# A wider slot block for the second expert of a pair in a mixture-of-experts layer

## The reference

```
logits = x @ router_w + router_b
top_val, top_idx = lax.top_k(logits, 2)
top_w = softmax(top_val)
for e in range(8):
    y = y + combine[..., e:e+1] * ((silu(x @ w_gate[e]) * (x @ w_up[e])) @ w_down[e])
```

## Time and profile before

| | before |
|---|---|
| median of 3 runs | 1698.21 us (1696.55 to 1700.08) |
| profiled execution, its own time | 1697.78 us |
| its span, first to last instruction | 1696.0 us |
| mean granted TensorE clock | 0.965 |
| PE busy | 1553.1 us (92%) |
| DVE busy / ACT busy | 398.8 us / 317.5 us |
| moved by DMA | 518.13 MB, 305 GB/s over the span |
| chain that ended last: PE / DMA / SP's queue | 46% / 18% / 4% |

### The profile page before, as it was taken

One profiled execution on the slowest core, in us unless ns is written; L12 is line 12 of the kernel. 1 busy time (PEld: TensorE's weight loads), 2 busy tenths in 40 slices (PEclk: granted clock), 3 DMA queues, 4 the chain that ended last, 5 costly groups with the idle time before them and its releaser, 6 DMA issues.

```text
span 1696.0 us, 33539 instructions
## 1 busy us (share of the span) xinstructions
PE 1553.1 (92%) x15321; PEld 1035.7 (61%) x15323; DVE 398.8 (24%) x781; ACT 317.5 (19%) x618; POOL 44.1 (3%) x83
## 2 busy tenths in 40 slices
PE   5996999979977999999999999988999899899986
PEld 4775788868765665766665656544565554565552
DVE  4666545465664300000000001000010000100002
ACT  3553444334541000100000001000010000000001
POOL 2010000010110000000000000000000000000000
PEclk8997899989987999999999999999999999999999
DMA  8523355356217898999999999999999999999994
GB/s 269 193 89 110 129 193 198 124 174 212 100 59 264 311 372 316 333 366 394 394 394 394 394 395 391 384 397 392 397 387 391 392 387 397 384 395 390 392 388 177
DMA packets 219575, 518.13 MB, mean 305 GB/s; under 512 B 6944, under 2 KB 8992, under 8 KB 219440
## 3 DMA queue, kind: packets, MB, share of 16 engines
q1 hardware_dynamic: 217248, 510.74, 81.0%
q0 software_dynamic: 1920, 5.31, 1.0%
q10 hardware_dynamic: 272, 0.00, 0.0%
HBM read 514.98 MB, written 1.05 MB: 304 GB/s over the span
## 4 chain that ended last, share of the span: by engine, by line
PE 46%; DMA 18%; SPq 4%; DVE 2%; issue 1%; ACT 0%; DVEq 0%; ACTq 0%
PE B L1844 23%; PE B L1859 16%; DMA ring<-in_moe_w_down_dram 16%; SPq L417 4%; PE B L1829 2%; PE B L1898 2%; DMA ring<-in_moe_w_up_dram 1%; PE B L1869 1%; DMA raw<-in_moe_w_down_dram 1%; PE B L1882 1%; PE B L1522 0%; PE B L1523 0%; PE B L1524 0%; DVE stats L891 0%; DVE acc L1455 0%
## 5 line engine op out<-in xcount | busy, mean ns | idle before, releaser
L1844 PE MATMUL B<-ring,xt 128*32 128x128 f32 (+1 forms) x5248 | 358.4, 325 | 15.4 <-DMA ring<-in_moe_w_up_dram 13.9
L1844 PE MATMUL B<-raw,xt 128*32 128x128 f32 (+1 forms) x4608 | 307.9, 322 | 19.7 <-DMA raw<-in_moe_w_up_dram 8.8
L1844 PEld LDWEIGHTS B<-ring,xt 128*32 128x32 f32 (+1 forms) x5248 | 247.0, 123 | 122.4 <-issue 24.0
L1844 PEld LDWEIGHTS B<-raw,xt 128*32 128x32 f32 (+1 forms) x4608 | 217.0, 122 | 109.4 <-issue 29.3
L1438 DVE TENSOR_TENSOR hact<-hact,B 128x256 f32<-128x256 f32 (+1 forms) x105 | 36.7, 383 | 884.1 <-ACT hact L799 884.1
L1859 PE MATMUL B<-ring,hidt 128*32 128x256 f32 (+1 forms) x1600 | 212.7, 479 | 17.9 <-DMA ring<-in_moe_w_down_dram 17.6
L870 DVE TENSOR_TENSOR wl<-raw,wh 128x1024 fp32r<-128x1024 f32 (+2 forms) x144 | 157.6, 1118 | 109.9 <-ACT wh L567 109.6
L1522 PE MATMUL B<-wh,xth 128*128 128x512 f32 (+1 forms) x416 | 168.6, 405 | 15.6 <-DVE wl L870 12.5
L1523 PE MATMUL B<-wl,xth 128*128 128x512 f32 (+1 forms) x416 | 163.9, 394 | 0.0
L1524 PE MATMUL B<-wh,xtl 128*128 128x512 f32 (+1 forms) x416 | 163.2, 392 | 0.0
L1859 PEld LDWEIGHTS B<-ring,hidt 128*32 128x32 f32 (+1 forms) x1600 | 75.7, 122 | 139.9 <-issue 104.0
(11 more groups left out here) (312 smaller groups left out, 947.2 us busy)
## 6 DMA issues: line engine op xcount, KB each, us to landing
ring<-in_moe_w_up_dram SPq DMA_DIRECT2D x46, 2048.0 KB, 19.7
ring<-in_moe_w_down_dram SPq DMA_DIRECT2D x44, 2048.0 KB, 19.5
raw<-in_moe_w_gate_dram SPq DMA_DIRECT2D x40, 2048.0 KB, 22.1
ring<-in_moe_w_gate_dram SPq DMA_DIRECT2D x30, 2048.0 KB, 20.7
raw<-in_moe_w_down_dram SPq DMA_DIRECT2D x26, 2048.0 KB, 19.1
raw<-in_moe_w_up_dram SPq DMA_DIRECT2D x24, 2048.0 KB, 19.8
raw<-in_w_in_dram SPq DMA_DIRECT2D x12, 2048.0 KB, 8.0
raw<-in_dense_w_gate_dram SPq DMA_DIRECT2D x5, 2048.0 KB, 7.7
```

What stands on the lines that cost most here:

```text
L1844: last = pe.matmul(bank[g * b.w:(g + 1) * b.w, o:o + b.cols], xt[:, k, b.c0:b.c0 + b.w], w[:, k, g * b.cols:(g + 1) * b.cols], start=k == ...
```

## The change

The second stream of PAIR gets a second block, of 32 slots, so that both streams have 96 slots in the same two blocks. The gather for a PAIR takes 192 columns in four banks, where it took 160 in three. The result takes bank 7 too, and the caps of streams 5 and 7 are 96 where they were 64.

```diff
-    CAPS = (96, 192, 32, 32, 96, 64, 96, 64)
+    CAPS = (96, 192, 32, 32, 96, 96, 96, 96)
...
         PAIR = Kind([[Block_(64, 0, 0, 0, 256, 0, 0, 4, 0), Block_(32, 64, 1, 0, 128, 1, 0, 5, 0, 64, 32)],
-                     [Block_(64, 96, 2, 0, 256, 2, 0, 6, 0, 0, 224)]],
-                    [[(0, 256, 0), (1, 128, 1)], [(2, 256, 2)]], (0, 1, 2), 3)
+                     [Block_(64, 96, 2, 0, 256, 2, 0, 6, 0, 0, 224), Block_(32, 160, 3, 0, 128, 3, 0, 7, 0, 64, 96)]],
+                    [[(0, 256, 0), (1, 128, 1)], [(2, 256, 2), (3, 128, 3)]], (0, 1, 2, 3), 2)
...
                 pick_stream(0, 96, first)
-                pick_stream(96, 64, second).then_inc(pick_done, 1)
+                pick_stream(96, 96, second).then_inc(pick_done, 1)
```

## The result

| | before | after |
|---|---|---|
| median | 1697.87 us (4 runs, 1696.55 to 1700.08) | 1526.4 us (4 runs, 1526.32 to 1529.08) |
| ratio | | 0.8993, 95% interval 0.8977 to 0.9008 |
| profiled execution / its span | 1697.78 / 1696.0 us | 1526.32 / 1524.2 us |

The kernel is 10.1% faster, 171.5 us by the medians. The forecast was 1527 us.

What follows compares the result with a forecast made beforehand. The prediction took transfers to bound the PAIR passes before and PE after. Start 1005.27, PAIR 253.52, one turn 246.49, tail 19.42 and 1.78 outside gave 1526.5, forecast as 1527 us, range 1514 to 1546.

Steps and rivals of the forecast that it cites:

- What bounds the kernel before: PAIR pass and both turns: transfers set the pace, 31.84 us a chunk against 27.76 us of PE work.
- The number of passes: Loop: 65 tokens over 64 slots cause the second turn; with 96 slots it goes, 225.20 us less.
- The wide chunk: Chunks of the two remaining PAIR passes: PE work rises 6.04 us to 33.80 us, and PE becomes the bound.
- SOLO's price: Added block of 32 behind a block of 64 in one unit: 1.96 us, the price the forecast took.
- The two prices: A block of 32 costs 1.96 us in SOLO or 1.77 us in a stream by itself; the cheaper makes chunks 33.23 us.
- What the waits absorb: PAIR chunks: 4.1 of the 6.0 us of added work fill waits, and 2.0 us a chunk lengthen the pass.
- Once a pass: Work once per PAIR pass after the change: gather 5.33 us, turned weights 2.77 us, scatter 7.1 us.
- The sum: Whole kernel: PAIR starts at 1005.27, then PAIR 253.52, one turn 246.49, tail 19.42, outside 1.78: 1526.5, so 1527 us.
- The first rival: PAIR passes: added blocks disappear in the waits and passes stay at the transfers' pace, 1474 us; chance 0.04.
- The second: PAIR passes: PE is the bound but waits for landings stay on top, 1556 us; chance 0.08.
- The third: Loop still turns twice and wide blocks are paid in three passes, 1778 us, 80 us slower; chance 0.02.
- The rate: Transfers in the two remaining PAIR stretches: down to some 350 to 370 GB/s.

Runs made afterwards that it cites:

- the cut in bytes: Down units of the PAIR passes load three of their four slices, PE work unchanged: 1654.19 us on the kernel before, 1527.91 us on the kernel after.
- the caps alone: Kernel before with only the caps changed and no added blocks, so expert 4's 65th token is left out: 1471.99 us, ratio 0.8664.
- the turned order: Kernel after with stream 1's blocks reversed (32 ahead of 64) on gate and up units: 1521.84 us, against 1527.08 us for the kernel after beside it.
- the turn put back: Kernel after with one more loop turn, empty of tokens: 1786.37 us, ratio 1.053.
- the kernel with the narrow PAIR: Kernel after with 64 slots again in the second stream of the PAIR pass ahead of the loop, the loop staying wide: 1500.03 us, ratio 0.8838.

## Why the prediction was right

- **What bounds the kernel before**: the transfers, shown by the cut in bytes, which moved the kernel before by 44 us and the kernel after not at all.
- **The number of passes**: 56 gate units, from the comparison of 65 with 96 instead of 64. With the caps alone the kernel takes 1471.99 us, where 1473 had been worked out. This is 226 us of gain before the cost.
- **The wide chunk**: 33.80 us forecast and 33.80 measured, 21.95 of gate and up, 10.90 of down and 0.96 of transposes. The choice of SOLO's price was right, since the added blocks stand in SOLO's order. The two prices, 1.96 and 1.77 us, were not two prices of the block: both hold changes between blocks of 64 and 32, in different number. With 0.14 us a change, as the turned order showed, I estimate 3.49 us for a block of 64 and 1.75 for one of 32 from the 18.03 and 21.53 us of four units, and TRIO's three changes then give 28.36 us for the 28.28 of the earlier trace rows. The rule of the Trainium skill that changes of tiling mode drain TensorE (TensorEngine Tiling (Array Packing), Tiling Modes) fits this, with 0.14 to 0.15 us a change here.
- **What the waits absorb**: the sum by stage was right, but the sentence that 2.0 us a chunk lengthen the pass holds only for a chunk that had waited 4.1 us. The PAIR became 27.7 us longer, about 4 us a chunk. PE's busy time rose by 41.8 us (211.85 to 253.62), and there were only 14.1 us of idle time to fill, since the PAIR's chunks from 1034.06 and 1061.82 us had taken 27.76 us each already, without a wait.
- **Once a pass**: the gather took 5.40 us for 5.33, the turned weights 2.77 for 2.77, the scatter 7.09 for 7.1.
- **The sum**: PAIR 253.62 us for 253.52, the turn 246.54 for 246.49, the tail 19.51 for 19.42, the start of the PAIR at 1004.53 for 1005.27. The last is the one term that missed: the added 0.86 us of the gather is there, and the stretch ahead of it was 0.8 us shorter (the landing before it let PE go at 985.02 us). That the total agrees to 0.6 us is luck in part: nine executions of the kernel after lie between 1521.33 and 1529.08 us.
- **The first rival** (the blocks vanish in the waits, 1474 us) failed on the size that had been given against it: 6.0 us of work for 4.1 us of wait a chunk. **The second** (landings still waited for) didn't occur: no landing lies in the chain of either pass, and 37 us less of transfers changed nothing. **The third** (two turns) didn't occur either, and its price of 1778 us was 8 us too low: the turn put back gave 1786.37, and 6.3 us of the difference are the stall, which the price had left out.
- **The rate**, forecast at 350 to 370 GB/s, was 378 in the PAIR and 308 in the turn. The two together make 344: the sum of the bytes was near, but more of them move in the first pass.

What the sum carried without naming it is the stall of the second turn, 12.77 us for the first gate unit and its waits in the kernel before, against 5.34 in the first turn. It went with that turn, since the turn left was built from PE's pieces alone. But hardly any of the 171.5 us are this stall. The last turn of the kernel with the caps alone has no stall and takes 220.68 us, and the second turn of the kernel before takes 222.06 with it. Where transfers set the pace they went on during the stall, and the next three chunks had no wait. Where PE sets the pace, as in the turn put back, all of it is paid.

## What to carry to other kernels

A cap that decides whether a whole pass runs is worth reading beside the counts that it meets: here one token over a cap of 64 cost 226 us, and 32 more slots in two passes cost 54 us. Price a widening per stage, from the idle time that the loaded engine has in the whole stage: of 41.8 us of added work in the PAIR 14.1 filled idle time, and the rest was paid in full. A chunk with a long wait shows more room than the stage has. Then widen only the stage whose count asks for it, which gave 27 us more, and put equal tile shapes next to each other. All of this is tuned to these counts: with others, where no cap is just exceeded, the wide blocks would be paid for nothing.

## What the runs showed of the hardware

- **The second turn of this loop starts with a stall on PE.** It appears in the kernel before (1455.59 us), in the kernel with fewer bytes and in the kernel with the turn put back, each time within the first gate unit of the second turn and never of the first. That unit then takes 12.77, 14.58 and 11.77 us, with two gaps of 3.13 and 2.23, 3.08 and 1.83, 2.37 and 1.97 us. Below are the kernel before, the kernel with the turn put back, and for comparison the first turn of the kernel after:

```profile
1455.59:1468.36 12.77, 7.41 (x98) 4.96 (x98) 0.69 (x1) 1.08 (x2) 0.00 (x0) 0.87 1.05 383
1510.39:1522.16 11.77, 7.43 (x98) 4.77 (x98) 1.29 (x2) 1.08 (x2) 0.00 (x0) 0.86 0.52 181
1258.15:1263.64 5.49, 5.49 (x98) 3.90 (x98) 1.29 (x2) 1.08 (x2) 0.00 (x0) 1.00 0.78 270
```

The trace calls the gaps issue: nothing that it shows was waited for. So the stall lies behind the jump back, one gap ahead of the first matmul and one after 14 to 23 records. Whether it is the loading of instructions was not tried, and its cause stays open. The trace's instruction queue moved three packets of 16 KB in the 12.77 us of the kernel before, against two in as long a stretch at the first turn, which doesn't settle it. Part of the cost is the clock. Behind the first gap it was at the lower of its two levels for part of the 4.31 us in which 23 records ran in the turn put back (mean 0.63), and for all of the 3.67 us of the first 14 records in the kernel before with fewer bytes (0.50). What the stall costs depends on the stage: 6.3 us where PE sets the pace, and 1.4 us (222.06 against 220.68, one trace each) where the transfers do, which ran on at 383 GB/s.

- **A change of tile width costs 0.14 to 0.15 us.** The same down unit takes 5.45 us behind a block of 32 and 5.30 us behind a block of 64. A gate unit of 96 slots takes 5.49 us behind a block of 32 and 5.34 us behind one of 64 (1258.15 us in the kernel after, 1231.00 us in the kernel with the narrow PAIR). And the turned order takes three changes out of four gate and up units for 0.42 us.
